# A table of distances for the chain's tokens in the projection blocks of a two-group encoder layer

## The reference

```python
h = _rms(x, lw['norm1_g'])
proj = h @ lw['w_in']
p_rwkv, q, k, v, qm, gates = jnp.split(proj, _split_points(IN_SIZES), axis=-1)
o_a, s_new, shift_new = _rwkv(p_rwkv, ...)              # per-token recurrence, 8 heads of 64
q, k = _rms(q, ...), _rms(k, ...)
o_b = _swa_prompt(q, k, v, lw['swa_sink'])              # banded attention with sinks and ALiBi
o_m = _mem_attend(_rms(qm, ...), mem_k, mem_v)          # attention into 256 memory tokens
br = jnp.einsum('btnc,ncd->btnd', jnp.stack([o_a, o_b, o_m], axis=2), lw['w_branch'])
x = x + jnp.sum(jax.nn.sigmoid(gates) * br, axis=2) @ lw['w_out']
a_in, u = jnp.split(_rms(x, lw['norm2_g']) @ lw['w_up'], 2, axis=-1)
x = x + (jax.nn.gelu(conv3(a_in)) * u) @ lw['w_down']
```

## Time and profile before

| | |
|---|---|
| median of three runs | 2237.29 us (2236.73 to 2246.06) |
| profiled execution | 2235.74 us, span 2233.9 us |
| TensorE busy | 2073.2 us (93%), granted clock 0.976 on average |
| VectorE busy | 1195.9 us (54%) |
| ScalarE busy | 961.5 us (43%) |
| GpSimd busy | 1137.1 us (51%) |
| mix blocks of groups 0, 1, 2 | 373.7, 377.5, 351.4 us |
| FFN blocks of groups 0, 1, 2 | 374.3, 373.4, 328.2 us |

### The profile page before, as it was taken

The page is one execution under the profiler, slowest core; times in us unless marked ns, Lnnn a source line. Parts: engine busy times, 40 slices in busy tenths (PEclk is TensorE's granted clock), DMA queues, the critical chain, the costliest instruction groups (busy, mean ns, idle before and its releaser), DMA issues. The chain is left out here.

```text
span 2233.9 us, 40378 instructions
## 1 busy us (share of the span) xinstructions
PE 2073.2 (93%) x15646; PEld 1928.5 (86%) x15646; DVE 1195.9 (54%) x2216; ACT 961.5 (43%) x1954; POOL 1137.1 (51%) x916
## 2 busy tenths in 40 slices
PE   5979999899999998999898999999989978899998
PEld 5868888799999987888788999999878867799998
DVE  5685545455664237654654466622765355457740
ACT  5423346445444432234563454444423456355542
POOL 5533333365666654333334566665533433567775
PEclk9999999999999999999999999999989989999999
DMA  5411123463334432112226433444311332644443
GB/s 166 148 62 59 64 86 104 137 205 112 126 127 160 142 111 85 49 54 86 86 97 207 145 124 123 132 151 145 104 57 49 105 111 87 198 152 147 147 157 124
DMA packets 158141, 264.04 MB, mean 118 GB/s; under 512 B 20096, under 2 KB 53120, under 8 KB 157952
## 3 DMA queue, kind: packets, MB, share of 16 engines
q1 hardware_dynamic: 157376, 260.42, 36.4%
q10 hardware_dynamic: 576, 1.05, 0.1%
HBM read 241.95 MB, written 19.46 MB: 117 GB/s over the span
## 5 line engine op out<-in xcount | busy, mean ns | idle before, releaser
L215 POOL TENSOR_TENSOR k_w_lo<-k_raw,k_w_hi 128x512 fp32r<-128x512 f32 x832 | 1090.0, 1322 | 1003.2 <-ACT k_w_hi L206 958.1
L206 ACT ACTIVATE k_w_hi<-k_raw 128x512 fp32r<-128x512 f32 x832 | 500.0, 617 | 386.0 <-PE k_acc L237 131.7
L235 PE MATMUL k_acc<-k_x_hi,k_w_hi 128*128 128x384 f32 (+1 forms) x1152 | 416.5, 362 | 14.6 <-PEq L70 10.0
L237 PE MATMUL k_acc<-k_x_hi,k_w_lo 128*128 128x384 f32 (+1 forms) x1152 | 382.0, 332 | 0.0
L236 PE MATMUL k_acc<-k_x_lo,k_w_hi 128*128 128x384 f32 (+1 forms) x1152 | 381.5, 331 | 0.0
L235 PEld LDWEIGHTS k_acc<-k_x_hi,k_w_hi 128*128 128x128 f32 x1152 | 221.6, 192 | 55.0 <-issue 28.5
L236 PEld LDWEIGHTS k_acc<-k_x_lo,k_w_hi 128*128 128x128 f32 x1152 | 222.3, 193 | 3.8 <-issue 1.2
L237 PEld LDWEIGHTS k_acc<-k_x_hi,k_w_lo 128*128 128x128 f32 x1152 | 221.1, 192 | 0.0
L235 PE MATMUL k_acc<-k_o_hi,k_w_hi 128*128 128x384 f32 (+1 forms) x288 | 97.9, 340 | 24.9 <-POOL k_w_lo L215 9.1
L235 PE MATMUL k_acc<-g0f_xg_hi,k_w_hi 128*128 128x384 f32 x352 | 118.6, 337 | 2.2 <-DVE g0fu_a_raw L2093 2.2
L235 PE MATMUL k_acc<-g1f_xg_hi,k_w_hi 128*128 128x384 f32 x352 | 117.9, 335 | 2.2 <-DVE g1fu_a_raw L2093 2.2
(11 more groups left out here) (747 smaller groups left out, 4386.8 us busy)
## 6 DMA issues: line engine op xcount, KB each, us to landing
k_raw<-w_up SPq DMA_DIRECT2D x264, 256.0 KB, 2.6
k_raw<-w_gate SPq DMA_DIRECT2D x144, 256.0 KB, 3.1
k_raw<-w_down SPq DMA_DIRECT2D x96, 256.0 KB, 3.7
k_raw<-w_rwkv SPq DMA_DIRECT2D x84, 256.0 KB, 2.9
k_raw<-w_branch SPq DMA_DIRECT2D x72, 256.0 KB, 3.5
k_raw<-w_attn SPq DMA_DIRECT2D x60, 256.0 KB, 2.7
k_raw<-w_out SPq DMA_DIRECT2D x48, 256.0 KB, 3.0
k_raw<-w_down_end SPq DMA_DIRECT2D x24, 256.0 KB, 3.2
```

The source lines that it names most:

```text
L206: act.activation(c.w_hi[s][:, 0:n], c.raw[s][:, 0:n], ACT.Copy).then_inc(c.hi_done, 1)
L215: pool.tensor_tensor(c.w_lo[s][:, 0:n], c.raw[s][:, 0:n], c.w_hi[s][:, 0:n].bitcast(F32), ALU.subtract).then_inc(c.lo_done, 1)
L235: pe.matmul(out, wh, xh, start=(u.begins and k == 0), stop=False)
L237: mm = pe.matmul(out, wl, xh, start=False, stop=(u.ends and k == u.kt - 1))
```

## The change

The written-out start and the even spread give way to a table: for each group and each token, how many half-steps are taken since the token before it. The instructions, the units and the tokens stay the same.

```diff
+DISTANCES = (
+    (2, 2, 2, 7, 0, 4, 4, 4, 4, 4, 0, 7, 4, 4, 3, 6, 1, 2, 2, 1, 5, 0, 0, 1, 1, 1, 2, 1, 1, 0, 2, 2, 2, 0, 2, 0, 0,
+     4, 2, 0, 2, 1, 1, 2, 2, 2, 0, 0, 2, 2, 0, 2, 0, 0, 4, 2, 0, 2, 1, 1, 2, 2, 2, 0, 0, 2, 2, 0, 2, 2, 1, 1, 1, 2,
+     1, 1, 2, 1, 1, 0, 0, 4, 0, 4, 0, 1, 3, 1, 0, 2, 1, 1, 2, 1, 1, 0, 0, 1, 0, 5, 1, 1, 4, 0, 2, 0, 0, 0, 1, 5, 1,
+     1, 2, 1, 1, 2, 0, 1, 1),
+    (12, 5, 4, 4, 4, 4, 0, 7, 4, 4, 3, 6, 1, 2, 2, 1, 5, 0, 0, 1, 1, 1, 2, 1, 1, 0, 2, 2, 2, 0, 2, 0, 0, 4, 2, 0,
+     2, 1, 1, 2, 2, 2, 0, 0, 2, 2, 0, 2, 0, 0, 4, 2, 0, 2, 1, 1, 2, 2, 2, 0, 0, 2, 2, 0, 2, 2, 1, 1, 1, 2, 1, 1, 2,
+     1, 1, 0, 0, 4, 0, 4, 0, 2, 2, 0, 0, 3, 2, 1, 4, 0, 1, 0, 0, 1, 0, 5, 0, 0, 4, 0, 2, 0, 0, 0, 1, 5, 1, 1, 2, 1,
+     1, 2, 0, 1, 0),
+    (13, 4, 4, 4, 4, 6, 0, 6, 4, 4, 4, 4, 3, 1, 2, 2, 5, 0, 0, 1, 0, 2, 1, 1, 2, 0, 2, 2, 1, 1, 2, 0, 0, 5, 1, 0,
+     2, 2, 2, 1, 1, 2, 0, 2, 1, 1, 0, 1, 0, 3, 2, 2, 2, 2, 2, 1, 1, 2, 0, 2, 1, 1, 1, 1, 0, 0, 4, 2, 1, 3, 0, 1, 0,
+     4, 0, 4, 0, 3, 1, 0, 0, 2, 1, 2, 3, 0, 1, 0, 0, 3, 0, 4, 1, 1, 4, 0, 2, 0, 0, 3, 0, 2, 3, 0, 1, 3, 0, 1, 0, 0,
+     0),
+)
+
+def at_distances(dense, distances):
+    order = []
+    for d in distances:
+        order += [0] * d + [1]
+    return order + [0] * (dense - sum(distances))
...
-        order = [0, 0, 1, 0, 0, 1, 0, 0, 1, 0, 0, 1] if g == 0 else [0] * 8
-        for m in range(2, R_TILES):
-            order += [0] * 4 + [1]
-        rest = n_scan + N_POST + N_ATTN_PREP + n_attn
-        order += [0] * 2 + [1] + [0] * 2 + [1]
-        order += spread(2 * len(us) - 4 * R_TILES - 4, rest)
+        order = at_distances(2 * len(us), DISTANCES[g])
```

## The result

The new kernel takes 2180.2 us (median of four runs, 2178.8 to 2184.0) beside 2237.0 for the kernel before: a ratio of 0.974, 95% interval 0.971 to 0.978, 57 us less. The forecast was 2191, 46 less, in a range of 2164 to 2228. The profiled execution took 2180.4 (span 2178.5). Two executions further down, one of e1_prep (2874.6) and one of the kernel before (10531.1), were in a slow state and are left out of every figure.

What follows compares the result with a forecast made beforehand. It took TensorE's waits for VectorE and ScalarE in the three mix blocks, plus half-level clock, as the bound; terms of 55.3 us less 9.0 for zero distances gave net 46, so 2237.3 to 2191, range 2164 to 2228.

Steps and rivals of the forecast that it cites:

- The case: Whole kernel: the forecast's case, moved tokens shrink TensorE's waits in the mix blocks, 30 to 66 us less, chance 0.55.
- scan of the decays: Preparation, L1282: scan moves ahead of a VectorE evacuation, saving 1.5, 1.5 and 2.0 us in groups 0, 1, 2.
- root of kk and its products: Preparation: Newton steps move ahead of an evacuation and their reader goes later, saving 4.5, 4.5 and 0 us.
- first power and later grams: Recurrence, L748: more half-steps cover the first power (1.7 each group); later pairs' grams move, saving 2.4, 2.4, 3.2 us.
- squares: Attention, L1139: ScalarE does nine squares in a row without splits between, saving 1.5, 1.5 and 4.0 us.
- first scores: Attention, L919: a gate's evacuation leaves the chain ahead of the scores, saving 1.0, 1.0 and 1.5 us.
- transposes: Attention, L969: first transposes of the probabilities get more cover or earlier bias, saving 0, 2.2 and 2.5 us.
- later memory scores: Attention, L932: values' tokens move two to four half-steps earlier, scores stay, saving 2.0, 2.0 and 3.0 us.
- The lower end: Lower bound of the root term in groups 0 and 1: 2.9 us a group, against 4.5 kept.
- zero distances: 99 tokens placed at the same half-step as the one before: new waits charged at 9.0 us, bounds 0 and 85.
- the clock: Granted clock returns from half level as waits shrink, mainly group 2's attention: 1, 1, 4 us, bounds 0 and 36.
- the waits pass on: Rival, whole kernel: removed waits reappear at the next token, only 19 us gained, about 2218; chance 0.22.

Runs made afterwards that it cites:

- e1_prep: Kernel before with only the tokens of the keys and the preparation moved to the new table's places: 2238.6 us, ratio 1.001.
- r_after: The new kernel run once more, unchanged, as the base for its neighbouring runs: 2184.0 us, ratio 0.977 to the kernel before.
- e6_split: The new kernel with 53 of its 99 zero distances taken apart by one half-step: 2202.6 us, ratio 0.985 to the kernel before.
- e8_root2: The new kernel's table with kk's second product and later tokens two half-steps later in groups 0 and 1, group 2 also respaced: 2183.1 us, ratio 0.973.

## Why the prediction was right, and where its steps were not

The case was the right one: most waits shrank by about what their half-steps cover, and the time fell, though by 57 and not by 46. The blocks of groups 0 and 1 took 362.0 and 362.5 us for the 361 and 363 forecast; the surplus is group 2's, 319.9 for 332. Point by point, in TensorE's waits, groups 0, 1, 2, of the new kernel's two profiles (the second is r_after):

| term | forecast | measured | second profile |
|---|---|---|---|
| scan of the decays | 1.5, 1.5, 2.0 | 1.9, 1.9, 1.4 | 1.9, 1.9, 1.4 |
| root of kk and its products | 4.5, 4.5, 0 | 0.5, 0.5, -0.6 | 0.5, 0.5, -0.6 |
| first power and later grams | 4.1, 4.1, 4.9 | 2.9, 2.9, 4.9 | 2.8, 2.8, 4.9 |
| squares | 1.5, 1.5, 4.0 | 1.5, 1.2, 4.6 | 1.3, 1.4, 4.8 |
| first scores | 1.0, 1.0, 1.5 | 1.7, 1.1, 1.5 | 1.7, -1.9, -1.3 |
| transposes | 0, 2.2, 2.5 | -1.2, -1.2, 0.8 | -1.4, 1.1, 1.1 |
| later memory scores | 2.0, 2.0, 3.0 | 2.9, 1.6, 3.7 | 2.9, 1.6, 3.7 |

- **Right**: scan, squares, memory scores, the first power, whose wait is gone in all three groups. Where the forecast measured by half-steps of 1.05 or 0.91 us of cover, the first power above all, that held, and L809 (before L788) stays at 2.7 as said, in group 2 it rises by 1.1.
- **Mis-sized: the later grams** of groups 0 and 1: their two waits fell by some 1.2 together, for 2.4.
- **Wrong: the root.** The working took VectorE's three Newton steps ahead of the evacuation and let two half-steps of cover follow. It did not let GpSimd's stretch move along: ScalarE waits there for the same row sums (7.01 us ahead of L305 at 861.25), so its weight splits (862.33), and behind them GpSimd's (863.03), start when the Newton steps start (862.97). Its "plain" 3.7 for the Newton steps also held two of them beside splits already (1.61 and 1.50). The lower end (2.9 a group) already assumed that none of the contention went, and it measured 0.5. Here the Trainium skill, page "SBUF — State Buffer", section "Who interferes with whom", weighed more than the forecast gave it: operations with two inputs from SBUF take 1.5 for 0.56 and those with one are untouched, as it says. And by its rule, all of them blocked, the term should have been at the lower end at best.
- **Wrong: the scores and transposes.** I gave L990 the cover of its own move. Later items, whose producers moved too, now wait 1.2 where they waited for nothing: two in group 1 and one in group 0, in the second profile one in each. And what L990 doesn't wait, L940 does: in groups 1 and 2 the two lines had 4.0 and 9.6 us together, and have 4.1 and 7.3 in one profile, 4.8 and 9.8 in the other. Why they trade between executions stays open.
- **Wrong in sign: the zero distances.** 9 us were charged for new waits. A new wait did come (L1011 in group 0, 2.2, in the second profile 0.3), but pairing the tokens saved 125 changes of tile shape, 12 to 16 us, and e6_split shows that the pairs are worth 0.3 us each.
- **Mis-sized: the clock.** I kept 4 of group 2's stretch, and that stretch alone gave 7, the preparation another 10. Its bounds, 0 and 36, held it. The forecast had a row for one of the two stretches only: the preparation's 0.80 is in none, and there the clock came back while the idle time stayed.

So the forecast of 46 came out of waits over-counted by 9 to 18 (49 before the charge, 40 after it, 31 measured), a clock under-counted by 6 to 11 (6 forecast, 12 over the span, 17 in the two stretches) and shapes, 12 to 16, not counted at all. The errors went partly against each other: that 46 came within 11 of the 57 is in part luck. Of the rivals, "the waits pass on" is true of the preparation (e1_prep), of the scores and transposes, and of what a better table can still do (e8_root2), not of the whole.

## What to carry to other kernels

Where two streams share TensorE by a written order, put chain tokens that can run together at one place: it saves the change between tile shapes and leaves the dense work behind them as cover for all the answers. Before moving a token away from a wait, look at what else its producer's engine releases at that moment: a queue that waits for the same event brings its backlog along. And compare variants by span times granted clock first: waits and shapes add up there, while the half level of the clock moves by 5 to 8 us between sets of runs of one kernel.

## What the runs showed of the hardware

A change between 128*128 matmuls and ones of 64*64, 64*128 or 128*64 costs TensorE about 0.1 us without any wait in the profile: in the mix blocks of groups 0 and 1 such a token starts 0.27 behind the last dense matmul in all three shapes, one of 128*128 0.17 to 0.18, and busy time at full clock falls by 0.13 for each change between the streams that goes. The Trainium skill, page "TensorEngine Tiling (Array Packing)", section "Key Properties", says that a change of the tiling mode drains the engine; the trace agrees in that the token starts later, and adds the price. I had not looked for it in the kernel before, where 386 such changes stood in the same view.

The granted clock of a stretch mostly went with the tokens of that stretch (0.78 with waits of 5.2, 3.6 and 4.4 in 47 us, 0.93 with 0.6, 2.1 and 3.7), but not by its idle time alone (0.80 with 12.6 us idle of 68, 0.95 with 11.3 of 67), and the same wait of 2.6 stood in stretches at 1.00, 0.95 and 0.92.
